# Hybrid decoder step on one core: meta tokens 12 and 13 moved to the end of the first norm's rows, and strips of 266 columns

## The reference, cut to what matters

```
h = rmsnorm(x); z = h @ w_in
u, cg, bg, q, k, v, o, gates, g_a, g_b = split(z)
a_out = bg * causal_conv3(cg * u)                  # A: needs the two rows before each output row
b_out = sigmoid(o) * mlstm(q, k, v, gates)         # first chunk: the 16 meta tokens
x = x + (sigmoid(g_a) * a_out + sigmoid(g_b) * b_out) @ w_out
x = x + (silu(conv3(up)[..., F:]) * conv3(up)[..., :F]) @ w_down    # F = 5632
y_prompt = rmsnorm(x) without the meta rows; y_sample = rmsnorm(x)
```

## Time and profile before

| | |
|---|---|
| median of three runs | 1702.03 us |
| the profiled execution, its own time | 1702.65 us |
| its span | 1700.9 us |
| granted TensorE clock, mean | 0.998 of full |
| PE busy | 1690.0 us, 99% |
| DVE busy | 1199.5 us, 71% |
| ACT busy | 766.8 us, 45% |
| POOL busy | 478.9 us, 28% |

### The profile page before, as it was taken

One profiled execution on the slowest core, in us unless ns is written; L12 is line 12 of the kernel. 1 busy time (PEld: TensorE's weight loads), 2 busy tenths in 40 slices (PEclk: granted clock), 3 DMA queues, 4 the chain that ended last, 5 costly groups with the idle time before them and its releaser, 6 DMA issues.

```text
span 1700.9 us, 37193 instructions
## 1 busy us (share of the span) xinstructions
PE 1690.0 (99%) x13726; PEld 1683.3 (99%) x13726; DVE 1199.5 (71%) x1901; ACT 766.8 (45%) x916; POOL 478.9 (28%) x501
## 2 busy tenths in 40 slices
PE   9999999999999999999999999999999999999997
PEld 8999999999999999999999999999999999999997
DVE  5875958668495866849688877777555777777554
ACT  6534435454443535444445555544333434334443
POOL 4432515232151523215333222222000222222220
PEclk9999999999999999999999999999999999999999
DMA  8788786868778686877776666666666666666663
GB/s 199 185 232 196 196 215 153 231 164 227 185 201 207 155 232 161 232 181 201 194 183 180 191 176 184 181 178 174 183 181 180 182 179 181 177 181 178 184 176 120
DMA packets 591165, 318.80 MB, mean 187 GB/s; under 512 B 17684, under 2 KB 585988, under 8 KB 588988
## 3 DMA queue, kind: packets, MB, share of 16 engines
q1 hardware_dynamic: 578564, 292.99, 64.0%
q10 hardware_dynamic: 10448, 21.57, 4.7%
q0 software_dynamic: 2064, 2.92, 0.8%
HBM read 305.09 MB, written 12.78 MB: 187 GB/s over the span
## 4 chain that ended last, share of the span: by engine, by line
PE 99%; ACT 0%; POOL 0%; DVE 0%; issue 0%; ACTq 0%; POOLq 0%; DVEq 0%
PE strip L1532 32%; PE strip L1524 32%; PE strip L1528 32%; PE aux L1403 1%; PE aux L1411 1%; PE strip L1455 0%; PE aux L1585 0%; PE aux L1475 0%; PE strip L1468 0%; PE aux L1615 0%; PE aux L1614 0%; PE aux L1628 0%; PE strip L1403 0%; PE aux L1619 0%; PE aux L1620 0%; PE aux L1612 0%
## 5 line engine op out<-in xcount | busy, mean ns | idle before, releaser
L982 DVE TENSOR_TENSOR w_lo<-w_raw,w_hi 128x1024 fp32r<-128x1024 f32 x556 | 720.4, 1299 | 309.3 <-ACT w_hi L713 308.7
L713 ACT ACTIVATE w_hi<-w_raw 128x1024 fp32r<-128x1024 f32 x557 | 586.5, 1059 | 751.8 <-PE strip L1532 710.2
L1524 PE MATMUL strip<-xh,w_hi 128*128 128x268 f32 (+1 forms) x2016 | 291.1, 286 | 0.0
L1532 PE MATMUL strip<-xh,w_lo 128*128 128x268 f32 (+1 forms) x2016 | 290.7, 286 | 0.0
L1528 PE MATMUL strip<-xl,w_hi 128*128 128x268 f32 (+1 forms) x2016 | 290.1, 286 | 0.0
L1532 PEld LDWEIGHTS strip<-xh,w_lo 128*128 128x128 f32 x2016 | 265.2, 188 | 0.4
L1524 PEld LDWEIGHTS strip<-xh,w_hi 128*128 128x128 f32 x2016 | 265.1, 188 | 0.2
L1528 PEld LDWEIGHTS strip<-xl,w_hi 128*128 128x128 f32 x2016 | 265.3, 188 | 0.0
L1524 PE MATMUL strip<-x2h,w_hi 128*128 128x266 f32 x1408 | 200.1, 284 | 0.0
L1528 PE MATMUL strip<-x2l,w_hi 128*128 128x266 f32 x1408 | 199.9, 284 | 0.0
L1532 PE MATMUL strip<-x2h,w_lo 128*128 128x266 f32 x1408 | 199.9, 284 | 0.0
(11 more groups left out here) (330 smaller groups left out, 1529.1 us busy)
## 6 DMA issues: line engine op xcount, KB each, us to landing
w_raw<-in_w_in SPq DMA_DIRECT2D x256, 512.0 KB, 4.5
w_raw<-in_w_up SPq DMA_DIRECT2D x176, 512.0 KB, 4.1
w_raw<-in_w_down SPq DMA_DIRECT2D x64, 512.0 KB, 4.0
w_raw<-in_w_out SPq DMA_DIRECT2D x32, 512.0 KB, 4.4
w_raw<-in_w_down SPq DMA_DIRECT2D x32, 384.0 KB, 3.4
out<-c_st ACTq DMA_DIRECT2D x8, 1024.0 KB, 7.0
c_st<-in_state_mlstm_C ACTq DMA_DIRECT2D x7, 1024.0 KB, 11.2
rb<-scratch_rows ACTq DMA_DIRECT2D x8, 270.0 KB, 5.1
```

Source lines behind the costliest of these rows:

```text
L713: act.activation(w_hi[:, slot, :], w_raw[:, slot, :], ACT.Copy).then_inc(hi_done, 1)
L982: v.tensor_tensor(w_lo[:, slot, :], w_raw[:, slot, :], w_hi[:, slot, :].bitcast(f32), ALU.subtract).then_inc(lo_done, 1)
L1524: pe.matmul(bank[b][:, 0:c1 - c0], w_hi[:, slot, w], rh[:, k0 + k, c0:c1], start=(first and k == 0), stop=False)
L1532: mm = pe.matmul(bank[b][:, 0:c1 - c0], w_lo[:, slot, w], rh[:, k0 + k, c0:c1], start=False, stop=(last and k == kk - 1))
```

## The change

The order of the 280 tokens becomes: meta 0 to 11, meta 14 and 15, the 256 prompt tokens, the 8 samples, then meta 12 and 13. With XM = 12, XF = 14 and XT = 278, the 266 rows that the mix needs are `xh[:, k, 12:278]`. Strips q, b, g_a, o and g_b use that range; u and c keep `12:280` and k and v keep `0:280`.

```diff
+    XM = C0
+    XF = XM + NMETA - M0
+    XT = XM + NM
...
-                    g.tensor_tensor(cu[:, :], us[:, :], cgs[:, :], ALU.mult).then_inc(cu_done, 1)
+                    g.tensor_tensor(cu[:, 0:M0 - C0], us[:, NM:NCU], cgs[:, NM:NCU], ALU.mult)
+                    g.tensor_tensor(cu[:, M0 - C0:NCU], us[:, 0:NM], cgs[:, 0:NM], ALU.mult).then_inc(cu_done, 1)
...
-            act.dma_start(x_tok[0:NMETA, 0, :], meta).then_inc(ends_in, 16)
-            act.dma_start(x_tok[T2:TL, 2, :], x_sample[:, 0, :]).then_inc(ends_in, 16)
+            act.dma_start(x_tok[0:C0, 0, :], meta[0:C0, :]).then_inc(ends_in, 16)
+            act.dma_start(x_tok[C0:XF, 0, :], meta[M0:NMETA, :]).then_inc(ends_in, 16)
+            act.dma_start(x_tok[SEQ + XF - 2 * P:XT - 2 * P, 2, :], x_sample[:, 0, :]).then_inc(ends_in, 16)
+            act.dma_start(x_tok[XT - 2 * P:TL, 2, :], meta[C0:M0, :]).then_inc(ends_in, 16)
...
             def take_kv(u, b, out, tail):
...
-                v.tensor_tensor(out, bank[b][:, 0:2 * P], rbc[:, 0:2 * P], ALU.mult)
-                v.tensor_tensor(tails[:, tail:tail + NT - 2 * P], bank[b][:, 2 * P:NT], rbc[:, 2 * P:NT], ALU.mult)\
+                e = 2 * P - M0 + XM
+                for o, lo, hi in ((0, 0, C0), (C0, XT, NT), (M0, XM, e)):
+                    v.tensor_tensor(out[:, o:o + hi - lo], bank[b][:, lo:hi], rbc[:, lo:hi], ALU.mult)
+                v.tensor_tensor(tails[:, tail:tail + XT - e], bank[b][:, e:XT], rbc[:, e:XT], ALU.mult)\
                  .then_inc(evacuated, 1)
...
-                        v.tensor_tensor(gz[:, :], gz[:, :], rbc[0:GR, :], ALU.mult).then_inc(g_step, 1)
+                        v.tensor_tensor(gabs[:, :], gz[:, :], rbc[0:GR, :], ALU.mult).then_inc(g_step, 1)
...
-                        v.tensor_scalar(gz[:, :], gz[:, :], b_col[:, :], None, ALU.add).then_inc(g_step, 1)
+                        v.tensor_scalar(gz[:, 0:C0], gabs[:, 0:C0], b_col[:, :], None, ALU.add)
+                        v.tensor_scalar(gz[:, C0:M0], gabs[:, XT:NT], b_col[:, :], None, ALU.add)
+                        v.tensor_scalar(gz[:, M0:NT], gabs[:, XM:XT], b_col[:, :], None, ALU.add).then_inc(g_step, 1)
...
-                    mix_strip(n, s, C0 if s == 0 else 0, NT, spread_r if first and s == 2 else None)
+                    mix_strip(n, s, XM if s == 0 else 0, XT if s == 0 else NT, spread_r if first and s == 2 else None)
...
-                    mix_strip(n, s, C0, NT)
+                    mix_strip(n, s, C0, NT if (s - 4) % 6 < 2 else XT)
```

More of the change, by code:

```diff
@@ L1077, in front @@
                                                op0=ALU.mult, op1=ALU.min).then_inc(g_step, 1)
-                        take(u0 + 1, 0, q_t[:, :], M0, NM)
+                        take(u0 + 1, 0, q_t[:, :], XM, NM)
                     if first and i == 4:
@@ L1127, in back @@
                 hs = n * HST
-                last = {9: (us, C0, NCU), 11: (cgs, C0, NCU), 13: (bs, M0, NM), 15: (ga, M0, NM), 17: (go, M0, NM),
-                        19: (gb, M0, NM)}
+                last = {9: (us, C0, NCU), 11: (cgs, C0, NCU), 13: (bs, XM, NM), 15: (ga, XM, NM), 17: (go, XM, NM),
+                        19: (gb, XM, NM)}
                 for i in range(8, HEAD_U):
@@ L1274, in out_four @@
                     v.wait_ge(x2g_step, m * 2 + 1)
-                    v.tensor_tensor(x2s[:, :], bank[q][:, 0:NM], tile_of(xres, m, M0, NT), ALU.add)\
+                    v.tensor_tensor(x2s[:, :], bank[q][:, 0:NM], tile_of(xres, m, XM, XT), ALU.add)\
                      .then_inc(evacuated, 1)
@@ L1278, in out_four @@
                     v.tensor_scalar(tile_of(x2h, m, MX, MX + NM), x2s[:, :], col(1, m), None, ALU.mult).then_inc(x2g_step, 1)
-                    v.tensor_scalar(tile_of(xres, m, M0, NT), x2s[:, :], 1.0, None, ALU.mult)
+                    v.tensor_scalar(tile_of(xres, m, XM, XT), x2s[:, :], 1.0, None, ALU.mult)
                     v.wait_ge(x2g_step, m * 2 + 2)
@@ L1314, in _ @@
                             step(n, 8, u0, 2 * q)
-                            take(n * 8 + (u0 + 2 * q + 1), q, zs[:, z, :], 0, NM, 0)
+                            take(n * 8 + (u0 + 2 * q + 1), q, zs[:, z, :], 0, NM)
                             v.wait_ge(evacuated, out_of(n * 4 + (s0 + q)))
@@ L1349, in _ @@
                             m = n * 4 + q
-                            v.tensor_tensor(tile_of(xres, m, NMETA, NT), bank[q][:, 0:NF], tile_of(xres, m, NMETA, NT),
+                            v.tensor_tensor(tile_of(xres, m, XF, XT), bank[q][:, 0:NF], tile_of(xres, m, XF, XT),
                                             ALU.add).then_inc(evacuated, 1)
@@ L1432, in turn_x @@
                         part(k, 1)
-                    pe.wait_ge(ends_in, 16 * 2)
+                    pe.wait_ge(ends_in, 16 * 4)
                     for k in range(lo, hi):
@@ L1454, in first_hi @@
                     for t, xt in enumerate((xh, xl)):
-                        mm = pe.matmul(bank[s][:, 0:NT - c0], w_hi[:, 2 * s + k // KU, w], xt[:, k, c0:NT],
+                        mm = pe.matmul(bank[s][:, 0:c1 - c0], w_hi[:, 2 * s + k // KU, w], xt[:, k, c0:c1],
                                        start=(k == 0 and t == 0), stop=False)
@@ L1467, in first_lo_part @@
                     pe.wait_ge(xh_done, k + 1)
-                    mm = pe.matmul(bank[s][:, 0:NT - c0], w_lo[:, 2 * s + h, (k - h * KU) * P:(k - h * KU + 1) * P],
-                                   xh[:, k, c0:NT], start=False, stop=(last and k == KT - 1))
+                    mm = pe.matmul(bank[s][:, 0:c1 - c0], w_lo[:, 2 * s + h, (k - h * KU) * P:(k - h * KU + 1) * P],
+                                   xh[:, k, c0:c1], start=False, stop=(last and k == KT - 1))
                 return mm
```

22 lines of the change are left out of this document (11 added, 11 removed).

## The result

The kernel after the change takes 1707.74 us (median of seven runs, 1705.75 to 1708.31), beside 1702.03 before (1701.14 to 1703.12). The ratio is 1.003 with a 95% interval of 1.002 to 1.0039. A second series, eleven runs on another chip, gave 1706.37 beside 1702.99: ratio 1.0022 (1.0013 to 1.0031). The profiled execution took 1706.36 us with a span of 1704.6 us, 3.7 more than the span before (1700.9). The forecast was 1699.4 us, 1697.8 to 1702.9.

What follows compares the result with a forecast made beforehand. The prediction took PE, busy 99%, as the bound, with waits for DVE's `w_lo` in five heads. From the profiled 1702.65 us, -1.44 (columns) and -1.20 (waits) gave 1700.0, so a median of 1699.4 us, range 1697.8 to 1702.9.

Steps and rivals of the forecast that it cites:

- Start: Loads at the kernel's start: two more DMAs on ACT's queue cost 0, at most 1.0 us if they landed last.
- Fewer columns: PE's strips q, b, g_a, o, g_b: 144 units of 266 instead of 268 columns save 10 ns each, -1.44 us.
- Rival E: PE's units of 266 `xh` columns may still take 2.930 us; only the waits go, -1.20, 1700.8 us; chance 0.11.
- `cu` in two pieces: POOL in round one of a head: DVE's L1160 comes between the pieces, PE's waits for `w_lo` vanish, -1.20 us.
- Rival B: DVE and POOL keep their old order of turns; waits grow 0.17 us in six heads, 1702.5 us; chance 0.22.
- `take_kv` and the gates: DVE's 48 added operations, 7.7 us, are hidden in the fronts; head 0's gate rows go out about 0.45 us later.
- the new order: DVE's L1160 between POOL's two `cu` pieces: 0.6 us gained in head 0's tight stretch, cancelling the later gate rows.
- What PE can keep: Heads waiting for DVE's `w_lo`: if the wait stays, 80 ns of faster units are lost in each of six, 0.48 us.
- The rest: `xres` at another offset and `take` at column 0, on engines with time to spare: 0.

Runs made afterwards that it cites:

- b5: Kernel before, with POOL's `cu` as two operations (2 and 266 columns) and nothing else; 1703.20 us beside 1702.54, ratio 1.0005.
- b8_114_rows: Kernel before, with SP's first four prompt loads of 114 rows instead of 112 and the meta load of 14 instead of 16; 1703.56 us beside 1702.10.
- b1: Kernel before, with only strips q, b, g_a, o and g_b reading 266 columns instead of 268; 1702.76 us beside 1702.54, ratio 1.0003.
- c1: Kernel after, with 112-row prompt loads for tile 0 again and `xh` and `xl` moved 12 bytes on; 1702.16 us beside 1702.89 before.
- a1: Kernel after, with tile 0's prompt rows loaded as 112 by SP and two by another small ACT DMA; 1704.21 us beside 1702.54 before.
- b6_dve_pieces: Kernel before, with DVE's takings of k and v in four pieces instead of two and the gates' bias in three; 1702.76 us beside 1702.54.
- b7: Kernel before, with the meta rows loaded by three DMAs of ACT's queue (12, 2, 2 rows) instead of one of 16; 1701.93 us beside 1702.10.
- b3: Kernel before, with strips b, g_a, o, g_b computing 266 columns from another start in each head; ran once, 3.000 us a unit from 13, 2.920 from 11.

## Why the prediction was wrong, step by step

- *Start, "I take 0".* This is the step that cost most. It measured +1.5 us (114 rows alone) to +1.7 us (all loads). I looked at when ACT's small DMAs would land and not at SP's prompt loads, whose row counts the diff changes from 112 and 16 to 114 and 14. The Trainium skill ("DMA: Bandwidth & Descriptors", How many engines (k)) has the rule: a transfer is shared by the largest number of engines up to 16 that divides its outer count. By it, as an estimate from that page, 112 rows go to 16 engines and 114 to 6. The rows on SP agree in sign (three loads hold it for 5.47 us instead of 2.65), and the increments do in number: 16 for a load of 112 rows, and 7 for one of 114, of which one comes at the issue and six are left.
- *Fewer columns, "10 ns, since that row has the same width and the same start within 16 bytes".* This failed in sign: -10 ns became +10 ns. A start "within 16 bytes" is just what does not carry over, as 2.900 to 3.000 us for one width show. Rival E had named the pitch, with 2.930; the truth lay outside its bounds too. I had bounded the price below by zero without a reason.
- *`cu` in two pieces, -1.20.* Rival B's mechanism was right: the order stays. In the earlier trace rows POOL's next operation begins as the last one ends (169.72 + 0.77 = 170.49, `kv` at 170.44), and yet I took L1160's being ready as enough to come between two of them. It was not: the stretch grew by 0.14 us, and the waits came in heads 0, 1, 2, 4 and 5. B's price for a head (0.17) was near what the split costs alone (b5's heads 1 to 7 grew by 1.1 us); B's time of 1702.5 us was too low all the same, for it had 10 ns a unit as a gain and nothing for the start.
- *`take_kv` and the gates.* Hidden in heads 1 to 7, as forecast. In head 0 the gates took 0.37 us longer (0.45 forecast), and the new order that was to cancel it did not come. Against PE they were 0.8 us later (L1091 begins 3.01 us ahead of head 0; L1081, the same step in before, began 3.84 ahead), since with the loads of 114 rows alone they are 0.34 later too (3.50 in b8_114_rows); with the waits after it head 0 grew by 0.8 us.
- *What PE can keep.* The reasoning held, and worked with the sign turned: a slower unit ahead of a wait is free, a faster one is lost. By this b1 cost less than 142 x 10 ns = 1.4 us, and c1 gained 2.4 us on a1 (1.67 above before, 0.73 below) and not 5.1. The forecast for c1 had counted 1.6 us of waits and so came to 3.5; its longer head 0 took part of the rest.
- *The rest* held: after head 7 the two traces take the same time.

The sum by parts: loads 1.7, `cu` 0.7, columns 0.2, DVE's pieces 0.2, so 2.8 of the 3.4 us measured beside before on one chip; each part is uncertain by more than what is left. By the traces, the loads' 2.1 us, 0.25 more by the end of head 0 and 1.0 in heads 1 to 7 make up the whole. Why the median of the first seven runs was 5.7 above, and not 3.4, stays open. My range of 1697.8 to 1702.9 was too narrow since it took no cost for the start, though a row count in the diff changed.

## What to carry to other kernels

Treat a changed row count of a DMA as a change of its speed, and look at what is queued behind it on its queue. Do not carry a matmul's pace from one tensor to another to within 1%: where the moving rows begin was worth up to eight times what I had put on two columns, and where the weights lie four times for one tensor and nothing for the other; measure it, and try a few offsets. Where PE waits in a tight stretch, take an operation out of the stretch of the engine that it waits for: one line was worth more here than the whole change.

## What was not expected of the hardware

- 24 matmuls of 266 fp32r columns take 2.900 to 3.000 us by the start of the moving rows alone, repeating every 32 bytes (with rows 1120 bytes apart), and 256 columns take longer than 258 (2.840 and 2.800). With the weights 32 bytes on, 2.920 becomes 2.960 for `x2h`, and nothing changes for `xh`. The cause inside the chip was not found.
- 268 columns at the same addresses took 2.980 us in seven units of head 0 and 2.930 later, in the kernel before, and 2.930 in head 0 of b6_dve_pieces; with 266 columns head 0 of b1_266_only had 2.930 to 2.950.
- A POOL operation on 2 columns took 1.03 us beside a DVE `w_lo`, and one on 266 columns 0.76 right after it; DVE's operation, ready since 169.97, came after both.
- The gate rows' way to DRAM and back took 9.2 to 11.3 us from the first DMA's issue to the first use (49.20 to 58.38 in b7, 48.10 to 59.37 in b3), in one and the same code. Since head 1 follows the gate rows' return to within 1.2 us, much of the scatter between runs of one kernel may be this; it was not tested.
